# A hybrid decoder step on one Trainium2 core: the first gate/up group of each FFN in plain products instead of a seven-product block scheme

## What is computed

```
def rmsnorm(x, g):
    xf = x.astype(jnp.float32)
    y = xf * lax.rsqrt(jnp.mean(xf * xf, axis=-1, keepdims=True) + EPS)
    return (y * g.astype(jnp.float32)).astype(x.dtype)

def swiglu(x, w_gate, w_up, w_down):
    return (jax.nn.silu(x @ w_gate) * (x @ w_up)) @ w_down
...
    x = x + 0.5 * swiglu(rmsnorm(x, n_f1), f1_g, f1_u, f1_d)
...
    x = x + 0.5 * swiglu(rmsnorm(x, n_f2), f2_g, f2_u, f2_d)
```

## Time and profile before

| | |
|---|---|
| median of 3 runs | 3441.51 us (3439.97 to 3444.74) |
| the profiled execution | 3437.6 us, of which the span of the profile is 3435.8 us |
| PE busy | 3254.9 us of the span |
| DVE, ACT, POOL busy | 1553.3, 1156.9, 1171.9 us |
| first FFN | first matmul at 27.04 us, end of its last down part near 822 us |
| second FFN | first matmul of its first group at 2611.09 us |

### The profile page before, as it was taken

The page is one execution under the profiler, slowest core; times in us unless marked ns, Lnnn a source line. Parts: engine busy times, 40 slices in busy tenths (PEclk is TensorE's granted clock), DMA queues, the critical chain, the costliest instruction groups (busy, mean ns, idle before and its releaser), DMA issues. The chain is left out here.

```text
span 3435.8 us, 53628 instructions
## 1 busy us (share of the span) xinstructions
PE 3254.9 (95%) x19758; PEld 3157.5 (92%) x19758; DVE 1553.3 (45%) x2470; ACT 1156.9 (34%) x1774; POOL 1171.9 (34%) x820
## 2 busy tenths in 40 slices
PE   7999999998999799999999999879997999999997
PEld 6999999998999699999999998769997999999997
DVE  7554445444777433333333333333325554445443
ACT  5222222225222354444454454321123222222224
POOL 3433333335122333323333333211234433343344
PEclk8999999999999899999999999779999999999998
DMA  2111111113222212112112121354410111111111
GB/s 84 56 49 37 49 49 49 37 49 110 76 83 83 82 52 69 58 51 69 58 51 75 52 66 39 92 198 145 133 38 25 55 50 37 49 47 51 37 49 59
DMA packets 274443, 222.89 MB, mean 65 GB/s; under 512 B 12042, under 2 KB 251786, under 8 KB 274288
## 3 DMA queue, kind: packets, MB, share of 16 engines
q1 hardware_dynamic: 273988, 220.56, 21.1%
q10 hardware_dynamic: 324, 0.41, 0.0%
HBM read 170.66 MB, written 50.28 MB: 64 GB/s over the span
## 5 line engine op out<-in xcount | busy, mean ns | idle before, releaser
L512 POOL TENSOR_TENSOR ffn_w_lo<-g_w_raw,ffn_w_hi 128x512 fp32r<-128x512 f32 x392 | 519.4, 1340 | 659.2 <-ACT ffn_w_hi L772 659.2
L709 PE MATMUL ffn_bank<-ffn_h,ffn_w_hi 128*128 128x368 f32 x1936 | 646.9, 334 | 35.7 <-POOL ffn_w_lo L512 20.4
L209 PE MATMUL mix_bank<-mix_h_hi,mix_w_hi 128*128 128x368 f32 x1752 | 639.0, 365 | 7.2 <-DVE mix_pre L2199 3.2
L711 PE MATMUL ffn_bank<-ffn_h,ffn_w_lo 128*128 128x368 f32 x1936 | 643.0, 332 | 0.0
L710 PE MATMUL ffn_bank<-ffn_h,ffn_w_hi 128*128 128x368 f32 x1936 | 638.2, 330 | 0.0
L210 PE MATMUL mix_bank<-mix_h_lo,mix_w_hi 128*128 128x368 f32 x1752 | 580.1, 331 | 0.0
L211 PE MATMUL mix_bank<-mix_h_hi,mix_w_lo 128*128 128x368 f32 x1752 | 579.2, 331 | 0.0
L1266 POOL TENSOR_TENSOR mix_w_lo<-g_w_raw,mix_w_hi 128x1024 fp32r<-128x1024 f32 x73 | 185.4, 2540 | 780.6 <-ACT mix_w_hi L1261 780.6
L709 PEld LDWEIGHTS ffn_bank<-ffn_h,ffn_w_hi 128*128 128x128 f32 x1936 | 367.7, 190 | 41.4 <-POOL ffn_w_lo L512 22.3
L772 ACT ACTIVATE ffn_w_hi<-g_w_raw 128x512 fp32r<-128x512 f32 x392 | 237.0, 626 | 455.6 <-PE ffn_bank L211 172.6
L209 PE MATMUL ffn_bank<-ffn_mid_hi,ffn_w_hi 128*128 128x368 f32 x1056 | 355.5, 337 | 22.8 <-POOL ffn_w_lo L512 18.2
(11 more groups left out here) (262 smaller groups left out, 4867.5 us busy)
## 6 DMA issues: line engine op xcount, KB each, us to landing
g_w_raw<-in_w_in SPq DMA_DIRECT2D x73, 512.0 KB, 5.5
g_w_raw<-in_ffn_w_gate SPq DMA_DIRECT2D x44, 512.0 KB, 4.1
g_w_raw<-in_ffn_w_down SPq DMA_DIRECT2D x44, 512.0 KB, 4.6
g_w_raw<-in_ffn_w_up SPq DMA_DIRECT2D x42, 512.0 KB, 4.7
scratch_qkv<-mix_out SPq DMA_DIRECT2D x24, 552.0 KB, 2.8
turn_kq<-scratch_qkv SPq DMA_DIRECT2D x32, 256.0 KB, 4.1
scratch_x<-g_x SPq DMA_DIRECT2D x8, 552.0 KB, 6.9
scratch_z<-turn_z_out SPq DMA_DIRECT2D x8, 552.0 KB, 2.8
```

Of the source, the lines that this page charges most:

```text
L209: pe.matmul(out, w_hi, x_hi, start=first, stop=False)
L512: pool.tensor_tensor(self.lo[:, k, :, :], self.source(i, g, pair, name), self.hi[:, k, :, :].bitcast(F32), ALU.subtract).then_inc(self.lo_ ...
L709: pe.matmul(bank[k][:, 0:TH], w_hi, hi, start=first and kc == 0, stop=False, skip_group_check=True)
L711: mm = pe.matmul(bank[k][:, 0:TH], w_lo, hi, start=False, stop=kc == KC // 2 - 1, skip_group_check=True)
```

## The change

1. The first group of each FFN no longer uses the block scheme. Thirds 0 and 1 get plain products too: for f1 the steps Za1, Zb1, Ta1, Ua1, Tb1, Ub1, for f2 Ua2, Ub2, Za2, Zb2, Ta2, Tb2, each for "g" and "u" (T is third 0, U third 1, Z third 2; a and b are the feature halves). That is 24 steps instead of 22. The first group's gate/up operands are the eight blocks B11 to B22 of both pairs; T1 to T4 and B22x fall away there.
2. All four blocks of h are made in chunks (`CHUNKS`, 16 of them). The sums S1 to S4 are made in the same group beside the products, and PE waits for all of them (`blk_lo`) once, ahead of the second group.
3. In the last group PE waits for "d 10" at the start of the down parts and for "d 11" at the fifth part.
4. The loads of the second group's first gate block and of `a1` and `a0` wait for splits of the new operands; counters of banks and steps are changed to fit.

```
+PLAIN_STEPS = tuple(f"{third}{half}{f}" for f, order in ((1, ("Za", "Zb", "Ta", "Ua", "Tb", "Ub")), (2, ("Ua", "Ub", "Za", "Zb", "Ta", "Tb")))
+                    for third, half in order)
+PLAIN_BLOCK = {"Za": "Z1", "Zb": "Z2", "Ta": "A11", "Tb": "A12", "Ua": "A21", "Ub": "A22"}
+PLAIN_BANK = {"T1": (0, 0), "U1": (1, 0), "T2": (2, 0), "U2": (1, 1)}
...
-              "A12": (14, 15), "A22": (16, 17)}
+              "A12": (14, 15), "A22": (16, 17), "A21": (9, 7)}
...
-            self.ops = by_turns(("B11", "B21")) + [("g", "B12"), ("g", "B22"), ("u", "B12"), ("u", "B22")]
-            self.ops += by_turns(("T2", "T3", "T1", "T4", "B22x")) + DOWN_OPS
-            self.steps = by_turns(("Z1a", "Z1b", "P1", "P2")) + [(p, n) for p in "gu" for n in ("Z2a", "Z2b")]
-            self.steps += by_turns(("P6", "P7", "P5", "P4", "P3"))
...
+            self.ops = by_turns(("B11", "B21", "B12", "B22")) + DOWN_OPS
+            self.steps = by_turns(PLAIN_STEPS)
+            self.sums = []
+            self.mids = ("Z1", "11", "21", "22", "Z2", "12")
+            self.used_up = {"B11": "Ua1", "B21": "Ub1", "B12": "Ta2", "B22": "Tb2"}
...
+        CHUNKS = (("A11", 0), ("A11", 1), ("A11", 2), ("A11", 3), ("A21", 0), ("A21", 1), ("A12", 0), ("A21", 2), ("A12", 1),
+                  ("A21", 3), ("A12", 2), ("A12", 3), ("A22", 0), ("A22", 1), ("A22", 2), ("A22", 3))
...
             load(0, 0, ("u", "f2"))
-            after(0, 0, "u", "T4")
+            after(0, 0, "g", "B21")
             load(0, 1, ("g", "f1"))
+            after(0, 0, "u", "B21")
             load(0, 0, ("d", "a1"))
-            after(0, 0, "g", "B22x")
+            after(0, 0, "g", "B22")
             load(0, 0, ("d", "a0"))
...
+            def plain_step(pair, name):
+
+                third_name, half, f = name
+                blk = PLAIN_BLOCK[third_name + half]
+                k, use = plain_bank(pair, third_name + f)
+                op = f"B{1 + (half == 'b')}{f}"
+                w.wait_lo(pe, 0, 0, pair, op)
+                if half == "a":
+                    freed(pe, 0, 0, k, use)
...
             for pair, name in FIRST.steps:
-                step(0, 0, pair, name)
+                plain_step(pair, name)
             down(0, 0)
+            pe.wait_ge(blk_lo, len(CHUNKS) + len(SUM_BLOCKS))
...
-            w.wait_lo(pe, 0, GROUPS - 1, "d", "11")
+            w.wait_lo(pe, 0, GROUPS - 1, "d", "10")
             for at, b in enumerate(THIRD_ORDER):
                 mid_wait(0, GROUPS - 1, b)
                 for c in range(KC):
+                    if at == 0 and c == KC // 2:
+                        w.wait_lo(pe, 0, GROUPS - 1, "d", "11")
                     down_part(0, GROUPS - 1, c, b, KC * at + c)
```

More of the change, by code:

```diff
@@ L685, in _, with products @@
                     fac.sum(pe, bank[b], b)
[L687 to L701, removed]
+            def products(k, blk, r, first, arrived=None):
                 for kc in range(KC // 2):
[L703 to L706, removed]
+                    if arrived is not None:
+                        arrived(kc)
                     hi, lo = slot(blk, 0, kc), slot(blk, 1, kc)
@@ L790, in gate_from_sum, with gate_plain @@
                 act.activation(mid(hid, name), mid(hid, name), ACT.Silu).then_inc(silu_done, 1)
+            def gate_plain(name):
+                third_name, done = {"11": ("T1", "Tb1"), "21": ("U1", "Ub1"), "22": ("U2", "Ub2"), "12": ("T2", "Tb2")}[name]
+                k, _ = plain_bank("g", third_name)
+                stepped(act, 0, 0, "g", done)
+                act.activation(mid(hid, name), bank[k][:, 0:TH], ACT.Silu).then_inc(free[k], 1)
             def gate_third(i, g, name):
@@ L824, in first_group @@
+                gate_third(0, 0, "Z1")
                 split_hi(0, 0, 5)
+                gate_plain("11")
                 split_hi(0, 0, 6)
-                gate_third(0, 0, "Z1")
-                block_hi("A22")
+                gate_plain("21")
                 split_hi(0, 0, 7)
-                gate_from_bank(0, 0)
                 split_hi(0, 0, 8)
[L831 to L834, removed]
+                for name in ("Z1", "11", "21"):
+                    mid_high(0, 0, name)
@@ L835, in first_group @@
+                gate_plain("22")
+                act.wait_ge(combo, 4)
+                act.wait_ge(blk_lo, len(CHUNKS))
+                for name in SUM_BLOCKS:
+                    block_hi(name)
+                mid_high(0, 0, "22")
+                gate_third(0, 0, "Z2")
+                mid_high(0, 0, "Z2")
                 split_hi(0, 0, 9)
-                act.wait_ge(blk_lo, last(LO_ORDER, "A22"))
                 split_hi(0, 0, 10)
-                block_hi("S1")
-                act.wait_ge(combo, 4)
@@ L984, in up_bank, with up_plain @@
                 dve.sem_inc(up_done, 1)
+            def up_plain(name):
+                third_name, done = {"11": ("T1", "Tb1"), "21": ("U1", "Ub1"), "22": ("U2", "Ub2"), "12": ("T2", "Tb2"),
+                                    "Z1": ("Z1", "Zb1"), "Z2": ("Z2", "Zb2")}[name]
+                k, use = plain_bank("u", third_name)
+                stepped(dve, 0, 0, "u", done)
+                if name[0] == "Z":
+                    dve.wait_ge(z_scaled, int(name[1]))
+                else:
+                    freed(dve, 0, 0, *((k - 3, use + 1)))
+                out = mid(hid, name)
+                dve.tensor_tensor(out, bank[k][:, 0:TH], out, ALU.mult).then_inc(free[k], 1)
+                freed(dve, 0, 0, k, use + 1)
+                dve.sem_inc(up_done, 1)
             def up_sum(i, g, name):
@@ L1049, in _ @@
             raw(0)
-            for k in range(1, KC):
+            for k in range(1, KC // 2):
                 raw(k)
-                block_lo("A11" if k <= KC // 2 else "A12", (k - 1) % (KC // 2))
-            block_lo("A12", KC // 2 - 1)
+                chunk_lo(k - 1)
+            chunk_lo(3)
+            raw(4)
+            chunk_lo(4)
+            chunk_lo(5)
+            raw(5)
+            chunk_lo(6)
+            chunk_lo(7)
+            raw(6)
+            chunk_lo(8)
+            chunk_lo(9)
```

171 lines of the change are left out of this document (78 added, 93 removed).

## The result

The changed kernel takes 3392.07 us (median of 4 runs, 3390.55 to 3393.46); the kernel before took 3440.74 in the runs beside it. The ratio is 0.9858, with a 95% interval of 0.9841 to 0.9875: 48.7 us less. The forecast was 3395 in a range of 3386 to 3407. The profiled execution took 3393.46 us, its span 3391.8.

What follows compares the result with a forecast made beforehand. PE, busy 3254.9 of 3435.8 us, was taken as the bound, with time lost in its waits and slow clock. Gains 19.7 + 20.4 + 3.2 + 3.2 = 46.5 us gave a forecast median of 3395 us, range 3386 to 3407.

Steps and rivals of the forecast that it cites:

- The first group of the first FFN: Group end forecast at 106.98 instead of 126.69, with waits and slow clock removed: 19.7 us gained.
- The bill of 24 matmuls: Two more steps in each first group, all on PE at 0.1668 us a matmul: 4.0 us more per FFN.
- The wait at A21: First group, PE waits for the fourth chunk's low part of A21 from DVE: 1.3 us of new wait.
- The bank wait of 0.6 us: First group, before Ua2 of the up pair: PE waits for DVE's third up product, ending at 60.6; 0.6 us.
- the slack: End of the first group, behind the load of `a0`: down operands and products ready only one to two microseconds early, no wait.
- The first group of the second FFN: Group end forecast at 2688.94 instead of 2709.37, by the first FFN's reckoning: 20.4 us gained.
- the end of the fourth step: Second FFN, first group: put 4.0 us behind 2618.79, at 2622.79; 26.5 us counted as lost behind it.
- The last group: PE starts down parts earlier, but POOL's norm additions end the stage: 3.2 us gained per FFN, not PE's 6.5.
- DVE and POOL as the bound of the first group: The two engines exclude each other throughout, so gate/up ends at 86.5 instead of 82.7: 3404 us, chance 0.20.
- The norm's chain as no bound: Last group: POOL's additions don't hold the end, PE's 6.5 us come through twice: 3386 us, chance 0.08.
- ACT in front of "d 00": First group: ACT's wait for a late `a0` load holds its queue and delays PE: 3413 or 3456 us, chance 0.02.
- Waits that only move: First groups: new waits behind chunks of h as long as the old, some 20 us; no change, 3441 us, chance 0.02.

Runs made afterwards that it cites:

- third run: Changed kernel with the 12 matmuls of the steps Tb2 of both pairs run twice in each first group: 3410.82 us, ratio 0.9915 to the kernel before.
- sixth run: Changed kernel with the split of "g B12" on POOL behind twelve chunks of h instead of eight: 3388.07 us, ratio 0.9855 to the kernel before.
- second run: Changed kernel without its last-group part, PE waiting for "d 11" ahead of all down parts as before: 3393.01 us, ratio 0.9868 to the kernel before.
- The first: Kernel before with only the change's last-group wait ("d 10" at the start, "d 11" at the fifth part): 3433.43 us against 3439.36, ratio 0.9987.
- fifth: Changed kernel with every second addition to the norm's sum moved from POOL to DVE: 3382.16 us against 3437.72 for the kernel before, ratio 0.9831.
- eighth runs: Changed kernel with POOL's clearing of the norm's sum moved ahead of its last two splits: 3387.65 us, ratio 0.9854 to the kernel before.

## Why the prediction was right, point by point

**The first group of the first FFN.** Forecast 19.7 us, measured 20.2. The bill of 24 matmuls holds, by the third run. The wait at A21 was there as worked out, 0.89 us instead of 1.3, and by the sixth run it has the cause that was charged: a split beside a product of h (2.01 us instead of 0.98, where 1.2 us were charged for each of three). The bank wait of 0.6 us was not there: the third up product ended at 59.54 instead of 60.6, and PE's list shows no wait for it. `a0` landed at 61.2 instead of 63.2 (3.9 us by the DMA's median instead of 4.6), and DVE stood idle for 4.79 us ahead of Zb2: the slack was about 4 us and not one or two. Third 0's low part came at 85.97, forecast 86.0.

**The first group of the second FFN.** Forecast 20.4, measured 19.5; that this is so near is in part luck, since errors of both signs nearly cancel. The prediction took the end of the fourth step as 24 matmuls at full clock behind 2618.79. In that profile only 15 matmuls ran in those 4.0 us, at clock 0.62; the nine missing ones are 1.5 us that it counted as lost behind the step:

```profile
2618.79:2622.79 4.00, 4.00 (x15) 4.00 (x16) 4.00 (x5) 1.29 (x3) 1.88 (x1) 0.62 0.00 0
```

It took the Z steps' wait as unchanged, 2.41 us. PE waited 0.85 us there instead and ran at clock 1.00 behind that. The wait ends with a split on POOL, "g B21", and beside DVE's work this split and the next took 3.52 us instead of 5.00, before and after:

```profile
2615.67 5.00 POOL L512 TENSOR_TENSOR ffn_w_lo<-g_w_raw,ffn_w_hi 128x512 fp32r<-128x512 f32 x2 [5.38 <-ACT ffn_w_hi L772]
```

```profile
2595.77 3.52 POOL L518 TENSOR_TENSOR ffn_w_lo<-g_w_raw,ffn_w_hi 128x512 fp32r<-128x512 f32 x2 [5.53 <-ACT ffn_w_hi L802]
```

On the other side it said that no matmul of 0.51 us would be left behind the Z steps, and that the group would end 66 us behind the fourth step. Both held in the first FFN only. In the second the chunk wait was 2.06 us, and the 53 matmuls in the 10.49 us behind it would take 53 x 0.1668 = 8.8 us at full clock: 1.7 us lost; the group ended 68.6 us behind the step. The longer chunk wait is the shorter Z wait over again: the chunk comes 18.3 us after the group's first matmul here and 18.5 in the second run, where the Z steps waited 2.05 us and the chunk wait was 0.89:

```profile
2607.91 0.44 PE L709 MATMUL ffn_bank<-ffn_h,ffn_w_hi 128*128 128x368 f32 x1 [0.89 <-DVE ffn_h L950]
```

In that run the clock stayed at 1.00 behind both waits, and the group took 77.37 us.

**The last group.** Forecast 3.2 us in each FFN, measured 3.2 and 3.9, and by the edit alone 3.1 in each. PE's wait for "d 11" is 1.38 us (1.2), PE saves 6.55 (6.5), and the rest falls to the norm's chain. The first, second, fifth and eighth runs show it from four sides: with the edit, without it, with a shorter chain, with an earlier start of it.

**The sum.** 46.5 us forecast for the profiled executions, 39.7 + 7.1 = 46.8 found in the FFNs, from which the mixer took 3 in this profile. The profiled spans differ by 44.0 us and the medians by 48.7; the executions of the kernel before lie between 3437.83 and 3444.74 us, those of the kernel after between 3390.55 and 3393.46. The 2 us by which the medians exceed the stages are inside that, and the median so came out 2.9 us under the forecast without a cause that a profile shows.

**The rivals.** DVE and POOL as the bound of the first group: against it stand 7.1 us for 48 matmuls, PE busy for all of the 34.63 us behind the chunk wait, and DVE's idle 4.79 us. The norm's chain as no bound: excluded. ACT in front of "d 00": a real mechanism, 8.6 us for a load 9.6 us late, but without its condition here. Waits that only move: 0.89 and 2.06 us did, of some 20 in each group.

What stays open is why a wait of 2.0 to 2.9 us is followed by the lower clock in one profile and not in another; no run was made for that.

## What to carry to other kernels

Where one group pays for setting up a cheaper scheme, count its own waits against the work that the scheme saves there: here 24 matmuls more (4.0 us) bought away some 24 us of waits and slow clock. When PE is made faster at the end of a stage, look at once for the serial chain behind it, here one engine's additions into one buffer. And compare stages, not totals, when two edits differ by a few microseconds: the mixer, which no edit touches, moved by 4.6 us between nine profiles, and by 6 us more in a tenth, for waits that only this run shows.

## What the runs showed of the hardware that was not expected

- **The length of a wait alone did not decide PE's clock.** In the first FFN of the kernel after, a wait of 2.54 us was followed by a granted clock of 1.00 (2.4 GHz). In the third run, at the same place, 2.07 us were followed by matmuls at the lower level (1.2 GHz). In the first groups of all ten profiles, waits of 0.78 to 1.72 us were followed by full clock, waits of 3.38 us and more by the lower level, and those of 2.01 to 2.85 us by either. In the first FFN the Z steps' wait ends 9.8 us after the group's first matmul in nine of the ten, so a longer wait there only means that the matmuls ahead of it were done sooner. The first matmul behind the wait, in the third run's timeline:

```profile
37.22 0.50 PE L709 MATMUL ffn_bank<-ffn_h,ffn_w_hi 128*128 128x368 f32 x1 [2.07 <-POOL ffn_w_lo L518]
```

- **One and the same weight split took 1.58 and 4.90 us.** These are the two first groups of the kernel after (within the 3.52 and 6.84 us above), beside DVE's work on h; the shortest splits take 1.3 us. PE's wait ends with it, so PE's wait in the Z steps changes with it.
- **One run made the mixer slower without touching it.** The third run's mixer took 1791.1 us, with six waits of about 2 us that no other profile has; the other nine took 1780.1 to 1784.7. The cause is open.
